# A first mixer reordered: low parts placed by hand, the inverse before the last convolutions, a weighted rotation, and the last product's end

## The reference

```python
u = rms_norm(concat([meta (16 tokens), x (256 tokens)]), norm_mix_pre)
proj = u @ w_in            # dq dk dv dz | b a | aq ak av
# delta rule group, 4 heads of 128, chunks of 64, forward and backward:
q, k, v = silu(short_conv(dq, dk, dv))     # 5 taps
uw = triangular_solve(I + strict(k k^T * decay * beta), [v*beta, k*beta*exp(gc)])
o  = scan over chunks (state 128x128 per head);  o_dn = rms_norm(o, o_norm) * silu(dz)
# attention group, 8 query heads and 2 key heads of 64:
q = rope(rms_norm(aq, q_norm)) / 8;  k = rope(rms_norm(ak, k_norm))
o_at = softmax(q k^T) av
mix = concat([o_dn, o_at]) @ w_out
h = h + rms_norm(mix, norm_mix_post);  u = rms_norm(h, norm_mlp_pre)   # then the first MLP
```

## Time and profile before

| | |
|---|---|
| median of 3 runs | 1111.14 us (1110.87 to 1112.1) |
| profiled execution: time | 1115.0 us |
| its span | 1113.2 us |
| TensorE, VectorE, ScalarE, GpSimd busy | 95%, 58%, 51%, 7% of the span |
| first mixer, to its product's end | up to 254.9 us |
| step to the first MLP | 254.9 to about 271 us |

### The profile page before, as it was taken

The page is one execution under the profiler, slowest core; times in us unless marked ns, Lnnn a source line. Parts: engine busy times, 40 slices in busy tenths (PEclk is TensorE's granted clock), DMA queues, the critical chain, the costliest instruction groups (busy, mean ns, idle before and its releaser), DMA issues.

```text
span 1113.2 us, 17730 instructions
## 1 busy us (share of the span) xinstructions
PE 1062.2 (95%) x7413; PEld 965.6 (87%) x7413; DVE 641.9 (58%) x998; ACT 562.7 (51%) x1007; POOL 81.8 (7%) x73
## 2 busy tenths in 40 slices
PE   6997998999999999998999999998999999999997
PEld 5887987889999997887889999997999879999996
DVE  4696932477645466678786454456443466553544
ACT  6653243256544445665556344345676666443442
POOL 1040002010000000000110000000322210000000
PEclk9999968999999999999999999999999999999999
DMA  8332100044655545443344564655343325645641
GB/s 258 115 114 76 51 27 1 1 141 146 207 187 187 192 181 198 142 143 115 114 159 151 201 203 149 216 190 170 115 145 113 114 84 171 223 147 198 207 149 62
DMA packets 114976, 160.36 MB, mean 144 GB/s; under 512 B 3776, under 2 KB 99264, under 8 KB 114896
## 3 DMA queue, kind: packets, MB, share of 16 engines
q1 hardware_dynamic: 114896, 159.22, 43.0%
HBM read 158.16 MB, written 1.05 MB: 143 GB/s over the span
## 4 chain that ended last, share of the span: by engine, by line
PE 84%; DVE 8%; ACT 4%; issue 2%; POOL 1%; DMA 0%; SPq 0%; DVEq 0%; POOLq 0%; ACTq 0%
PE PS L642 23%; PE PS L644 22%; PE PS L643 22%; ACT SCR L1366 3%; DVE WL L1798 2%; PE PS L955 1%; PE PS L960 1%; POOL SM L2385 1%; PE PS L1327 1%; PE PS L676 1%; DVE SPARE L1798 1%; PE PS L1350 1%; PE PS L1248 1%; PE PS L1338 1%; DVE H L1834 1%
## 5 line engine op out<-in xcount | busy, mean ns | idle before, releaser
L1798 DVE TENSOR_TENSOR WL<-RAW,WH 128x1024 fp32r<-128x1024 f32 (+1 forms) x177 | 214.7, 1239 | 69.7 <-ACT WH L1366 69.4
L1366 ACT ACTIVATE WH<-RAW 128x1024 fp32r<-128x1024 f32 (+1 forms) x191 | 194.9, 1048 | 47.9 <-DMA RAW<-in_gu 27.0
L642 PE MATMUL PS<-UH,WH 128*128 128x256 f32 (+2 forms) x664 | 188.2, 283 | 4.2 <-DVE WL L1798 3.0
L644 PE MATMUL PS<-UH,WL 128*128 128x256 f32 (+2 forms) x664 | 187.5, 282 | 0.0
L643 PE MATMUL PS<-UL,WH 128*128 128x256 f32 (+2 forms) x664 | 187.4, 282 | 0.0
L1366 ACT ACTIVATE SCR<-PS 128x512 f32<-128x512 f32 (+8 forms) x233 | 100.9, 469 | 169.9 <-PE PS L644 115.9
L1798 DVE TENSOR_TENSOR SPARE<-RAW,SPARE 128x1024 fp32r<-128x1024 f32 x100 | 118.0, 1220 | 23.3 <-ACT SPARE L1366 23.3
L642 PEld LDWEIGHTS PS<-UH,WH 128*128 128x128 f32 (+1 forms) x664 | 124.6, 188 | 6.1 <-DVE WL L1798 3.5
L644 PEld LDWEIGHTS PS<-UH,WL 128*128 128x128 f32 (+1 forms) x664 | 124.7, 188 | 0.2
L643 PEld LDWEIGHTS PS<-UL,WH 128*128 128x128 f32 (+1 forms) x664 | 124.2, 187 | 0.9
L1892 DVE TENSOR_TENSOR SCR<-SCR,PS 128x512 f32<-128x512 f32 x34 | 23.4, 688 | 160.2 <-PE PS L644 109.0
(11 more groups left out here) (307 smaller groups left out, 2127.9 us busy)
## 6 DMA issues: line engine op xcount, KB each, us to landing
RAW<-in_gu SPq DMA_DIRECT2D x44, 1024.0 KB, 5.3
RAW<-in_dn SPq DMA_DIRECT2D x22, 1024.0 KB, 6.7
RAW<-in_w_up SPq DMA_DIRECT2D x16, 1024.0 KB, 5.9
RAW<-in_w_down SPq DMA_DIRECT2D x16, 1024.0 KB, 5.0
RAW<-in_a_qkv SPq DMA_DIRECT2D x12, 1024.0 KB, 5.4
RAW<-in_w_in SPq DMA_DIRECT2D x11, 1024.0 KB, 5.3
RAW<-in_kv_w SPq DMA_DIRECT2D x8, 1024.0 KB, 6.0
RAW<-in_w_out SPq DMA_DIRECT2D x4, 1024.0 KB, 4.8
```

The lines of the kernel that those rows point to most:

```text
L642: e.matmul(o, lh, rh, start=start, stop=False)
L644: return e.matmul(o, ll, rh, start=False, stop=stop)
L1366: return e.activation(o, i, func, bias=bias, scale=scale, accum_out=acc)
L1798: e.tensor_tensor(lo_of(n_), half_src(n_), hi_of(n_).bitcast(F32), SUB).then_inc(s_lo_dve, 1)
```

## The change

1. VectorE's `ahead` takes a lead; it stays 3 up to conv.3 and is 0 afterwards: low parts are placed one by one, by steps low.n in the lists and by the steps of z, q and og. The taps of the convolutions become steps of their own.
2. The lists are written anew: inv.2 to inv.12 stand before most of conv.5 to conv.11; z.2 and z.3 move from the output norm to the last part of stage 1, with their SiLU (zs) left in stage 2; VectorE's share of meta.2 follows that of inv.2.
3. The rotation uses tables that are multiplied by the norm weights once, on GpSimd.
4. All four last halves of `w_out` go through `out_last`; a list of its own (`BETWEEN_FIRST`) follows it, with the MLP's first halves spread over it, and 2 in place of 18 warming steps. The first MLP's first halves take the slots of `SPARE`.

```diff
 STAGE_1 = steps_of(
-    "ba gates.0 conv.0 conv.1 gates.1 conv.2 gates.2 conv.3 gates.3 silu.0 kv.0 kv.1 ktok.0 ktok.1 kv.2 kv.3 start.0 start.1 "
-    "meta.0 q.0 q.1 inv.0 meta.1 inv.1 q.2 q.3 q.4 rows.0 z.0 solve z.1 conv.4 inv.2 conv.5 inv.3 meta.2 inv.4 conv.6 inv.5 "
-    "meta.3 conv.7 inv.6 silu.1 vtok.0 rows.1 inv.7 meta.4 conv.8 inv.8 rows.2 conv.9 inv.9 vtok.1 vtok.2 inv.10 conv.10 "
-    "meta.5 inv.11 conv.11 inv.12 meta.6 silu.2 in.0 inv.13 in.1 gqa.0 inv.14 qp.0 gqa.1 qp.1 gqa.2 qp.2 gqa.3")
+    "ba gates.0 conv.0 conv.1 taps.1 gates.1 conv.2 gates.2 conv.3 taps.3 gates.3 silu.0 kv.0 kv.1 ktok.0 ktok.1 kv.2 kv.3 "
+    "start.0 start.1 meta.0 low.10 q.0 q.1 inv.0 low.11 q.2 inv.1 meta.1 low.12 q.3 q.4 solve z.0 low.13 z.1 conv.4 inv.2 inv.3 "
+    "meta.2 low.16 conv.5 rows.0 inv.4 inv.5 inv.6 meta.3 taps.5 inv.7 conv.6 low.17 inv.8 conv.7 low.18 rows.1 inv.9 meta.4 "
+    "taps.7 inv.10 silu.1 rows.2 inv.11 conv.8 rows.3 low.20 inv.12 vtok.2 meta.5 conv.9 vtok.0 in.0 taps.9 rows.4 inv.13 low.21 "
+    "conv.10 vtok.1 in.1 meta.6 low.22 conv.11 inv.14 taps.11 silu.2 z.2 gqa.0 qp.0 gqa.1 qp.1 qp.2 gqa.2 z.3 gqa.3")
 STAGE_2 = steps_of(
...
-    " on.0 z.2 on.1 z.3 on.2 og.4 on.3 og.5 on.4 og.6 on.5 og.7 on.6")
+    " on.0 on.1 low.26 og.4 zs on.2 low.27 og.5 on.3 on.4 low.28 og.6 on.5 on.6 low.30 og.7")
...
+BETWEEN_FIRST = steps_of(
+    "sq.0.0 mx.0.0 lo.2 sq.0.1 r0.0 mx.0.1 hi.3 ad.0.0 hs.0.0 ad.0.1 hs.0.1 lo.3 sq.1.0 r1.0 mx.1.0 xn.0.0 sq.1.1 r0.1 xn.0.1 "
+    "fe.0.0 mx.1.1 fe.0.1 ad.1.0 fe.0.2 ad.1.1 fe.0.3 hs.1.0 fe.0.4 hs.1.1 fe.0.5 r1.1 fe.0.6 xn.1.0 fe.0.7 xn.1.1 "
+    "fe.1.0 fe.1.1 fe.1.2 fe.1.3 hi.4 lo.4 fe.1.4 fe.1.5 fe.1.6 fe.1.7 hi.5 lo.5")
...
-WARM = {0: 14, 1: 18, 2: 2, 3: 18, 4: 2, 5: 18}
+WARM = {0: 14, 1: 2, 2: 2, 3: 18, 4: 2, 5: 18}
...
-                head = (0, 1, 4, 5, 2, 3, 6, 7, 4, 5)[:8 + (b - a) % 8]
+                head = (4, 5, 6, 7, 0, 1, 2, 3) if r == 2 else (0, 1, 4, 5, 2, 3, 6, 7, 4, 5)
...
-        z_bank = (4, 5, 2, 3)
+        z_bank = (4, 5, 1, 3)
...
+                        pe.wait_ge(*emptied[6 + d])
...
-            for k in range(2):
-                out_half(1, half_of(("out", 1, 0), k), k, mix_ready(1, k), False)
-            out_last(1, [half_of(("out", 1, 1), j) for j in range(2)], [2, 3], [mix_ready(1, 2), mix_ready(1, 3)])
+            out_last(1, [half_of(("out", 1, k // 2), k % 2) for k in range(4)], range(4), [mix_ready(1, k) for k in range(4)])
...
+                    ac.wait_ge(*me_o["k", 1])
...
+            def z_silu():
+                for h in (2, 3):
+                    ac.wait_ge(*z_a["x", h])
+                    act(ZT[:, h, :], ZT[:, h, :], ACT.Silu).then_inc(*z_a.step(h))
...
-            def ahead(n):
+            def ahead(n, by=AHEAD):
...
             def conv(i):
-                ahead(HALF_CONV[i])
+                ahead(HALF_CONV[i], AHEAD if i < 4 else 0)
+
+            def low(n):
+                ahead(n, 0)
...
-                for c, (x1, x2, a, b, cs, sn) in enumerate(tiles):
-                    e.tensor_tensor(a, x2, sn, MUL).then_inc(*gr_v.step((n, c, "a")))
-                    e.tensor_tensor(b, x1, sn, MUL).then_inc(*gr_v.step((n, c, "b")))
...
+            def rotate(n, i, x, t, nh):
+
+                w, wt = (y.rearrange("p c h (a s f) -> p c h a s f", a=2, s=2) for y in (x, t))
+                if i == 0:
+                    for c in range(2):
+                        for s in range(2):
+                            sn = SINW[n].rearrange("p c (a s f) -> p c a s f", a=2, s=2)[:, c, :, s, :]
+                            e.tensor_tensor(wt[:, c, :, :, s, :], w[:, c, :, :, 1 - s, :], bc(sn, nh, 1), MUL).then_inc(*gr_v.step((n, c, s)))
+                if i == 1:
+                    dv.wait_ge(*gr_v[n, 1, 1])
+                    e.tensor_tensor(x, x, bc(COSW[n], nh, 2), MUL).then_inc(*gr_v.step((n, "c")))
+                if i == 2:
+                    dv.wait_ge(*gr_v[n, "c"])
+                    e.tensor_tensor(x[:, 0:2], x[:, 0:2], t, ADD).then_inc(*gr_v.step((n, "s")))
...
-            ahead(LAST_OUT[1] + 1)
+            ahead(LAST_OUT[1] - 1)                           # VectorE; ScalarE: ahead(LAST_OUT[1])
...
+            for n in "qk":                                   # GpSimd, before ba
+                w = R[n + "_norm"].rearrange("p (a s f) -> p a s f", a=2, s=2)
+                cw, sw = (y[n][:, 0:2, :].rearrange("p c (a s f) -> p c a s f", a=2, s=2) for y in (COSW, SINW))
+                cs, sn = (C[y].rearrange("p (c a f) -> p c a f", c=2, a=2) for y in ("cos", "sin"))
+                for s in range(2):
+                    e.tensor_tensor(sw[:, :, :, s, :], sn, bc(w[:, :, 1 - s, :], 2, 1), MUL).then_inc(*gr_o.step((n, "s", s)))
+                    e.tensor_tensor(cw[:, :, :, s, :], cs, bc(w[:, :, s, :], 2, 1), MUL).then_inc(*gr_o.step((n, "c", s)))
+                po.wait_ge(*gr_o[n, "s", 0])
+                e.tensor_scalar(sw[:, :, :, 0, :], sw[:, :, :, 0, :], -1.0, None, MUL).then_inc(*gr_o.step((n, "n")))
+            e.tensor_copy(COSW["k"][:, 2, :], R["k_norm"]).then_inc(*gr_o.step("m"))
```

More of the change, by code:

```diff
@@ L66 @@
 STAGE_1 = steps_of(
[4 rows of a table removed]
[5 rows of a table added]
 STAGE_2 = steps_of(
-    " ".join(f"scan.0.{i} gqa.{2 * i + 4} scan.1.{i} gqa.{2 * i + 5}" for i in range(8)).replace("gqa.19", "gt") +
-    " on.0 z.2 on.1 z.3 on.2 og.4 on.3 og.5 on.4 og.6 on.5 og.7 on.6")
+    " ".join(f"scan.0.{i} gqa.{2 * i + 4} scan.1.{i} gqa.{2 * i + 5}" + f" low.{22 + i}" * (0 < i < 4) for i in range(8)
+             ).replace("gqa.19", "gt") +
+    " on.0 on.1 low.26 og.4 zs on.2 low.27 og.5 on.3 on.4 low.28 og.6 on.5 on.6 low.30 og.7")
 STAGE_3 = steps_of(
@@ L585, in program @@
         for r, early, late in ((2, gq_p["g"], mx_lo[1, 3]), (4, dt_p[3, 1], dh_u[7]), (6, None, sh_u[15])):
-            for i, x in ((2, early), (3, early), (6, late), (7, late)):
-                spare_free[MLP_AT[r][0] + i] = x
+            i, j = (0, 2) if r == 2 else (2, 6)
+            for k in range(2):
+                spare_free[MLP_AT[r][0] + i + k], spare_free[MLP_AT[r][0] + j + k] = early, late
         block = ctx.enter_context(nc.Block())
@@ L1651, in og @@
             def og(k):
-                ahead(half_of(("out", 1, k // 2), k % 2))
+                ahead(half_of(("out", 1, k // 2), k % 2) + (k == 6))
             def on(i):
@@ L1672, in _ @@
                                **{"in": gqa_in}))
-            in_order(STAGE_2, dict(scan=scan, gqa=gqa, gt=gqa_turn, z=z, on=on, og=og))
-            ahead(LAST_OUT[1] + 1)
+            in_order(STAGE_2, dict(scan=scan, gqa=gqa, gt=gqa_turn, zs=z_silu, on=on, og=og))
+            ahead(LAST_OUT[1])
             between(1)
@@ L1994, in every, with meta_blocks @@
                 return bc(m[0:p, 0:p], n, 1)
+            def meta_blocks():
+                dv.wait_ge(*me_p["t"])
+                for d in range(2):
+                    s = slice(4 * d, 4 * d + 4)
+                    e.tensor_tensor(MM[:, s, :].rearrange("p h (b j) -> p h b j", j=8),
+                                    bc(compact(XC)[0:16, d, 8:12, :], 2, 2),
+                                    bc(C["m8"][0:16, 0:16].rearrange("p (b j) -> p b j", j=8), 4, 1), MUL
+                                    ).then_inc(*me_v.step(f"e{d}"))
             def inv(i):
@@ L2131, in rows @@
                     dv.wait_ge(*gr_v["kn"])
-                    e.tensor_tensor(K_, K_, bc(bc(R["k_norm"], 2, 1), 3, 1), MUL).then_inc(*gr_v.step("kw"))
-                    rotate("k", K_, 2, gr_v["kw"])
+                    for j in range(3):
+                        rotate("k", j, K_, T1[:, 0:256].rearrange("p (c h e) -> p c h e", c=2, h=2), 2)
             def scan(d, i):
@@ L2189, in og @@
             def og(k):
-                ahead(half_of(("out", 1, k // 2), k % 2))
+                ahead(half_of(("out", 1, k // 2), k % 2), 0)
             def on(i):
@@ L2223, in on @@
                                                ).then_inc(*mx_lo.step((1, h)))
-            in_order(STAGE_1, dict(gqa=gqa, ba=ba, gates=gates, conv=conv, kv=kv, q=q, z=z, ktok=ktok, vtok=vtok, start=start, inv=inv, meta=meta,
+            in_order(STAGE_1, dict(gqa=gqa, ba=ba, gates=gates, conv=conv, taps=taps, low=low, kv=kv, q=q, z=z, ktok=ktok, vtok=vtok, start=start, inv=inv, meta=meta,
                                solve=solve, qp=qp, rows=rows))
-            in_order(STAGE_2, dict(scan=scan, gqa=gqa, gt=gqa_turn, z=z, on=on, og=og))
-            ahead(LAST_OUT[1] + 1)
+            in_order(STAGE_2, dict(scan=scan, gqa=gqa, gt=gqa_turn, low=low, on=on, og=og))
+            ahead(LAST_OUT[1] - 1)
             between(1)
```

96 lines of the change are left out of this document (39 added, 57 removed).

## The result

The changed kernel takes 1100.95 us (median of four runs, 1097.80 to 1103.71) beside 1111.45 us of the kernel before on the same chip: ratio 0.9901, 95% interval 0.9875 to 0.9927. The forecast was 1095, in a range of 1088 to 1107. So it is faster, by 10.5 us by the medians where 16 was forecast. The profiled execution took 1103.71 us, the slowest of the four, around a span of 1101.7, 11.5 less than the span of before.

What follows compares the result with a forecast made beforehand. TensorE, busy 95% of the span, was taken as the bound: its own work, stands and half-clock stretches. The terms summed to -17.3 us, 1.3 was given back for short waits: -16.0, so 1095 us, range 1088 to 1107.

Steps and rivals of the forecast that it cites:

- R1: Rival, end of stage 1: the clock stays down, 1105 us, or 1100 with part of it kept; chance 0.22.
- (a): Stage 1, before meta.2: stand of 4.0 us and 1.7 of slow clock go, -5.7; new stand before solve, +1.0.
- (b): Before vtok.0: 2.3 us stand and 1.7 of slow clock go; new waits at meta.5 and in.0; net -2.6 us.
- (d): End of stage 1: shorter stands around the norm sums of q, -1.5 us; z.2 and z.3 moved here, +5.9.
- (c): End of stage 1: convolutions, z.2 and z.3 among small steps raise the clock, -7.8 us (bounds 0 and -11.2).
- (e): Tail of stage 2: output norm without z.2 and z.3, -4.2 us; low parts 29 and 30, +1.0; net -3.2.
- (f): End of the mixer's product: shorter way to the next MLP's first turn, as after the first MLP; -3.4 us.
- (g): Rotation tables weighted on GpSimd: hidden behind TensorE, 0 on the path; up to 1.5 us on three low parts.
- (h): Moved low parts: same count of splits, 1.2 us each, halves 13 and 14 closest to their use; 0.
- (i): Added waits, TensorE's before meta.6's last products and ScalarE's before in.0, and the earlier WROW reload: 0.
- R2: Rival: low parts come late, TensorE standing 1.2 us before each of nineteen halves; +7, 1118 us; chance 0.08.
- R3: Rival: stage 1's waits only change place, (a), (b) and (d) give nothing; 1106 to 1110 us; chance 0.10.

Runs made afterwards that it cites:

- the second profile: The changed kernel, unedited, run and profiled once more beside three other kernels on one chip: 1102.63 us.
- z.0 first: The changed kernel with z.0 put ahead of the picker product (solve) again: 1097.97 us.
- the fastest version: The changed kernel with z.0 ahead of solve and conv.4's low part (low.13) ahead of solve's VectorE work: 1093.71 us.

## Why the prediction was right in sign and 6 us too low

The measured 1100.95 lies inside the stated range, but not in the band that the prediction held likeliest (1091 to 1099, 0.52): it lies in the one given to R1 (1099 to 1107, 0.22).

**(a)** The mechanism was right on both sides. The 4.0 us went, the stretch behind it took 3.73 instead of 5.47 us (1.74, forecast 1.7), and the new stand before solve is 2.30 (forecast 2.3). What failed is the sentence "A new stand of 2.3 in place of the 1.3 before z.0: +1.0 us". Steps (a) and (b) had each charged a stand of before with the slow clock behind it, and (a) put none behind this one. It cost 1.65 us on solve (4.84 against 3.19) and 1.6 on the three products behind it (10.56 us, against 8.95 with the gap filled), 3.3 in all; other small differences give 0.9 of it back. The gap filled to its length shows the cause and the size: 3.25 us.

**(b) to (d)** The stands are as walked: 0.8 + 0.9 for meta.5 and in.0 (forecast 1.3), 1.3 before qp.2 (forecast 1.4), none before z.2. "I leave two short spells of slow clock, as long as those behind today's two stands, 1.7 each" was mis-sized: they were two, but of 6.8 us at half clock. At the loss of 0.43 of the earlier trace rows that is 5.8 us instead of 3.4. z.3 ran in one of them, at 4.62 us where 3.05 was the price of z.2. The two waits of (b) are the other 0.4 of the 2.8. Taking z.2 and z.3 out again shows that the core of (c) is right: with them in place the clock is 0.82 over that part, without them it is 0.53 for 22 us.

**(e)** Right, and too small by 1.2: the 60 matmuls behind on.5 ran in 13.95 us without a stand, so the low parts 29 and 30 cost nothing where I had charged 1.0. The wait for the first split was 1.02 (forecast 1.0).

**(f)** 2.7 and, in the second profile, 3.0 us (4.53 to 1.84 and 1.56), forecast 3.4. Of the 1.3 us of half clock behind it only the first profile shows anything.

**(g)** Nothing on the path that the run of before with it alone could tell. **(h)** Nothing on the path as the change places the low parts; but "0" is not what the placing is worth: with solve moved up, it keeps 2.9 us of idleness and splitting out of VectorE's queue at the one place where TensorE waits for it, worth 4.8 us there. **(i)** No row shows either wait.

**The rivals.** R1 came true in part: the clock fell to half twice at the end of stage 1, but not throughout. R2 had its mechanism shown twice, by edits next to the change (2.39 us before conv.4, and the reverse of it with the lead restored), and not in the change itself. R3 and R4 are out: (a) and (b) brought what their stands were worth, and the clock did not stay up. The sum with what was measured: -17.3 + 0.2 (start) + 2.4 (a) + 2.8 (b to d) - 1.2 (e) + 0.7 + 1.3 (f) - 0.4 (rest) = -11.5, the difference of the spans. The sum was missed by 5.8 us: the clock took 7.0 (3.3 + 2.4 + 1.3), and everything else together gave 1.2 back, so the allowance of 1.3 for short waits was not needed. The 0.2 at the start is no effect of the change: in profiles of kernels that are the same up to there the first product begins anywhere from 18.06 to 19.11 us.

What stays open: why the clock falls behind a stand in one execution and not in another. The stand of 1.3 us before the norm sums was there in the changed kernel, with half clock behind it (2.72 us for the sums), and in z.0 first, where they took 1.95 us. The Trainium skill (TensorE: Matmul & The Clock Gate, "Part 4: PE-mode transpose") says that a transpose does not bring up the full clock, since it does not count as busy in the same way. No run here put plain products in the place of the turns alone, so it is neither borne out nor refuted: the spell behind 146 us shrank from 6.8 to 3.4 with 2.4 us of products among the turns, and also in kernels without them.

## What to carry to other kernels

When a change trades one stand of TensorE for another, charge the new one with the slow clock behind it as well, as the old one was; here a 2.3 us stand cost 5.6, and filling it with warming products of the right length gave 3.25 of that back. A weight product between the turns can be worth more than its cover of a wait: moving two of them back cost 4.5 to 6 us. And before a low part, or any work for later, is put at a place in a queue, ask who waits for what stands behind it: the same 1.2 us split cost a stand of 2.4 us behind solve's results and one of 0.2 ahead of them.

## What the runs showed of the hardware

Half clock came in pieces of about 3.4 us or of multiples of it, at different places in kernels with the same program up to there; 3.4 us of it costs about 1.6 (6.8 us of it: 3.25). The times of one kernel spread with it, over 5.5 to 6 us in the changed kernel and up to 9 in that before (spans from 1105.4 at a mean clock of 0.992 to 1114.3 at 0.981, on one chip), but over less than 1 in the fastest version, so that two versions less than 3 us apart should be told apart by the trace, stage by stage, not by a few medians.

GpSimd and VectorE held each other up where both read SBUF at once, and which of them paid differed. Here it was mostly GpSimd, building the tables beside VectorE's three splits, in the changed kernel:

```profile
19.67 1.30 POOL L2445 TENSOR_TENSOR SCR<-CST,ROWS 128x64 f32<-128x64 f32 x1
20.93 1.31 POOL L2446 TENSOR_TENSOR SCR<-CST,ROWS 128x64 f32<-128x64 f32 x1
22.20 1.31 POOL L2445 TENSOR_TENSOR SCR<-CST,ROWS 128x64 f32<-128x64 f32 x1
23.47 0.33 POOL L2446 TENSOR_TENSOR SCR<-CST,ROWS 128x64 f32<-128x64 f32 x1
```

```profile
19.50 3.83 DVE L1820 TENSOR_TENSOR WL<-RAW,WH 128x1024 fp32r<-128x1024 f32 x3 [0.45 <-ACT WH L1375]
```

The first three tables take 1.3 us each and end as the splits do; the fourth, of the same shape, takes 0.33. The splits take 3.83 us, against 3.57 in the kernel before: 0.26 for the three. In the kernel before the loss lay on VectorE as well: its two splits at 80.33 took 3.21 us with GpSimd at work, against 2.36. The Trainium skill (SBUF — State Buffer, "Who interferes with whom") calls it an exclusive lock and says that the order of issue decides who blocks. The trace fits that: at 19 us GpSimd waits for the end of each 1.2 us split.
